# Residual added in PSUM by matmuls with the identity, output stored by half rows

## What is computed

```
h = h + peer_ffn(rmsnorm(h, norm_ffn_g), w_q, subkeys, u, v)
out = rmsnorm(h, norm_final_g)

peer_ffn(x): scores of x @ w_q against two sets of 128 subkeys; top 16 of each;
             top 16 of their 256 sums -> experts, g = softmax(top scores)
             act[t,h,k] = gelu(x[t] . u[expert]) * g[t,h,k]
             y[t]       = sum over h,k of act[t,h,k] * v[expert]
rmsnorm(x, g): x * rsqrt(mean(x*x) + 1e-6) * g
```

## Time and profile before

| | |
|---|---|
| median of 3 runs | 2017.38 us (2014.5 to 2019.98) |
| profiled execution | 2018.92 us |
| its span in the profile | 2017.1 us |
| mean granted clock of TensorE | 0.983 |
| PE busy | 1955.8 us, 97% |
| DVE, ACT, POOL busy | 1341.7 (67%), 1011.5 (50%), 320.5 us (16%) |
| loads | 311.4 MB read, 155 GB/s over the span |

### The profile page before, as it was taken

The page is one execution under the profiler, slowest core; times in us unless marked ns, Lnnn a source line. Parts: engine busy times, 40 slices in busy tenths (PEclk is TensorE's granted clock), DMA queues, the critical chain, the costliest instruction groups (busy, mean ns, idle before and its releaser), DMA issues.

```text
span 2017.1 us, 34435 instructions
## 1 busy us (share of the span) xinstructions
PE 1955.8 (97%) x12338; PEld 1730.1 (86%) x12338; DVE 1341.7 (67%) x2732; ACT 1011.5 (50%) x1641; POOL 320.5 (16%) x138
## 2 busy tenths in 40 slices
PE   7998999999999999999999999999999999999998
PEld 6776787778778888999899999999999998888886
DVE  6357556656655558889787689933666766666666
ACT  5436546555554446666434455665444443333333
POOL 0000000000000000000000057886666610000000
PEclk9898999999999999999999999999999999999999
DMA  5242454433345553433333534454343445555554
GB/s 229 73 157 74 149 211 172 174 117 128 115 145 189 186 184 130 147 136 136 106 126 126 178 126 168 179 180 151 138 146 136 143 162 188 197 190 195 191 194 156
DMA packets 85150, 313.99 MB, mean 156 GB/s; under 512 B 9456, under 2 KB 9456, under 8 KB 84592
## 3 DMA queue, kind: packets, MB, share of 16 engines
q1 hardware_dynamic: 85040, 312.49, 44.2%
HBM read 311.40 MB, written 1.05 MB: 155 GB/s over the span
## 4 chain that ended last, share of the span: by engine, by line
PE 92%; DVE 5%; ACT 2%; issue 1%; DMA 1%; SPq 0%; DVEq 0%; ACTq 0%
PE ps L282 29%; PE ps L414 22%; PE ps L401 15%; PE ps L1783 5%; PE ps L2635 3%; PE ps L2341 3%; PE ps L736 2%; PE ps L1852 2%; PE ps L430 1%; PE ps L799 1%; DVE wsplit L266 1%; PE ps L810 1%; PE ps L2172 1%; PE ps L2160 1%; PE ps L2155 1%
## 5 line engine op out<-in xcount | busy, mean ns | idle before, releaser
L260 ACT ACTIVATE wsplit<-ring 128x1024 fp32r<-128x1024 f32 x572 | 603.9, 1057 | 478.4 <-PE ps L414 268.9
L266 DVE TENSOR_TENSOR wsplit<-ring,wsplit 128x1024 fp32r<-128x1024 f32 x438 | 535.0, 1224 | 328.9 <-ACT wsplit L260 327.6
L282 PE MATMUL ps<-hsplit,wsplit 128*128 128x256 f32 x5064 | 648.2, 287 | 5.2 <-DVE hsplit L698 2.1
L282 PEld LDWEIGHTS ps<-hsplit,wsplit 128*128 128x128 f32 x5064 | 622.6, 193 | 12.9 <-issue 5.5
L266 POOL TENSOR_TENSOR wsplit<-ring,wsplit 128x1024 fp32r<-128x1024 f32 x134 | 320.3, 2397 | 1302.2 <-ACT wsplit L260 1302.2
L414 PE MATMUL ps<-wsplit,gsplit 128*128 128x512 f32 x1992 | 456.5, 390 | 0.0
L414 PEld LDWEIGHTS ps<-wsplit,gsplit 128*128 128x128 f32 x1992 | 373.3, 188 | 81.4 <-issue 4.2
L401 PE MATMUL ps<-wsplit,hsplit 128*128 128x512 f32 x1248 | 308.8, 405 | 17.6 <-DVE wsplit L266 10.5
L401 PEld LDWEIGHTS ps<-wsplit,hsplit 128*128 128x128 f32 x1248 | 241.3, 196 | 70.3 <-issue 18.9
L1783 PE MATMUL ps<-hsplit,wsplit 128*128 128x256 f32 x936 | 128.5, 288 | 0.0
L1783 PEld LDWEIGHTS ps<-hsplit,wsplit 128*128 128x128 f32 x936 | 116.3, 191 | 0.0
(11 more groups left out here) (319 smaller groups left out, 1706.5 us busy)
## 6 DMA issues: line engine op xcount, KB each, us to landing
ring<-in_weights SPq DMA_DIRECT2D x580, 512.0 KB, 3.3
work<-in_tables SPq DMA_DIRECT2D x1, 2123.0 KB, 12.4
xT<-in_x SPq DMA_DIRECT2D x1, 1024.0 KB, 4.9
work<-in_subkeys SPq DMA_DIRECT2D x1, 1024.0 KB, 15.0
work<-in_decay SPq DMA_DIRECT2D x2, 512.0 KB, 4.1
out_x<-work SPq DMA_DIRECT2D x2, 512.0 KB, 2.6
work<-in_w SPq DMA_DIRECT2D x1, 512.0 KB, 5.7
ring<-in_gain_row SPq DMA_DIRECT2D x1, 512.0 KB, 3.5
```

The costliest lines, as they stand in the source:

```text
L260: act.activation(wsplit[:, n % RING, 0, :], slab(s), ACT.Copy).then_inc(S("split", "lead"), 1)
L266: eng.tensor_tensor(wsplit[:, n % RING, 1, :], slab(s), wsplit[:, n % RING, 0, :], ALU.subtract).then_inc(S("split", RESTS[stream][0]), 1)
L282: mm = pe.matmul(dst, wsplit[:, n, a, c * P:(c + 1) * P], hsplit[:, b, c, :], start=(c == 0 and t == 0), stop=(c == KC - 1 and t == 2))
```

## The change

In words: the two functions that turn x in the query stage go, with the two waits on their result (of TensorE ahead of the early slabs, of VectorE ahead of its copies to PSUM) and the view `x_rows`. `residual_tensor` opens two banks with zeros, as before, and then adds x to them by 8 float32 matmuls of a chunk of `xT` (stationary) with the identity. For the second 128 tokens (banks 2 and 3) it waits only for the last GELU, for the first 128 (banks 0 and 1) for the last product of `late_vector`. The last norm reads PSUM in place of the sum in SBUF: ScalarE's Square waits for the matmuls directly, VectorE's scaled product reads `YR`. Each half row of 512 is stored by itself, as soon as its product is done.

```diff
--- before.py
+++ after.py
@@ -151,7 +151,6 @@
     picks = sb("picks", [P, 3, T])
     root, rinv = picks[:, 0, :], picks[:, 1, :]
     act_in, gated = sq[:, 0:3, :], sq[:, 3:6, :]
-    x_rows = xT[:, :, :].rearrange("p (t a) n -> p t (a n)", t=TT)
     row_stats = sb("row_stats", [P, 3, TT])
     bounds = sb("bounds", [P, 7, HH])
     lbd, lbe = bounds[:, 0:2, :], bounds[:, 2:4, :]
@@ -2457,8 +2456,6 @@
                 norm_tensor(pe, pre, 0)
             if u == 4:
                 column_tensor(pe, pre, 0)
-        pe.wait_ge(S("norm", "column"), rinv_steps(pre) + 3)
-        x_rows_tensor(pe, pre)
         score(0, 5)
         turn(1, 6, pre="m5")
         turn(2, 4)
@@ -2495,7 +2492,6 @@
             score(0, u - 1)
             if u == 1:
                 root_scalar(act, "n5", 0)
-        x_rows_scalar(act)
         score(0, 5)
         turn(1, 6)
         turn(2, 4)
@@ -2513,7 +2509,6 @@
         return 3 + c % 3
 
     def early_tensor(pe, st, stream):
-        pe.wait_ge(S("final", "x_rows"), 1)
         with pe.Fori(0, EARLY // 6) as i:
             for k in range(6):
                 split_project(pe, ps[:, hidden_bank(k), 0:T], stream, 16 + k, i).then_inc(S(st, "hidden"), 1)
@@ -2554,7 +2549,6 @@
         for tt in range(TT):
             own(v.tensor_scalar(best[:, tt, 0:6, :], best[:, tt, 0:6, :], row_stats[:, 2, tt:tt + 1], None, ALU.mult))
 
-        v.wait_ge(S("final", "x_rows"), 1)
         v.tensor_copy(ps_iota, iota)
         v.tensor_copy(ps_key, best_at[:, :, :, :].rearrange("p t h k -> p (t h k)"))
         own(v.tensor_copy(ps_best, best[:, :, :, :].rearrange("p t h k -> p (t h k)")))
@@ -2706,9 +2700,11 @@
             pe.wait_ge(S(st, "act"), i * 6 + (k + 1))
             split_rows_output(pe, st, VALUES + k, k % 3, i)
 
+
+        pe.wait_ge(S(st, "gelu"), NKEYS)
+        residual_tensor(pe, 1)
         pe.wait_ge(S(st, "late"), NKEYS - EARLY)
-        for y in range(4):
-            pe.matmul(ps[:, y, :], zeros[:, :], zero_rows(), start=True, stop=False, skip_group_check=True)
+        residual_tensor(pe, 0)
         with pe.Fori(0, TURNS) as i:
             for k in range(6):
                 output(k, i)
@@ -2734,42 +2730,32 @@
                 rest_of(v, st, VALUES + 2 + k, i)
         step(0, NKEYS - 1)
 
-
-
-    def x_rows_tensor(pe, pre):
-        wait_h(pe, pre)
-        for tt in range(TT):
-            for c in range(KC):
-                mm = pe.transpose(YR[:, tt, c * P:(c + 1) * P], xT[:, c, tt * P:(tt + 1) * P], eye)
-        mm.then_inc(S("final", "x_turned"), 1)
-
-    def x_rows_scalar(act):
-        act.wait_ge(S("final", "x_turned"), 1)
-        act.activation(x_rows[:, :, :], YR, ACT.Copy).then_inc(S("final", "x_rows"), 1)
-
+    def residual_tensor(pe, tt):
+        for half in range(2):
+            pe.matmul(ps[:, 2 * tt + half, :], zeros[:, :], zero_rows(), start=True, stop=False, skip_group_check=True)
+        for c in range(KC):
+            pe.matmul(YR[:, tt, c * P:(c + 1) * P], xT[:, c, tt * P:(tt + 1) * P], eye, start=False, stop=False,
+                      skip_group_check=True)
 
 
 
     def final_vector(v):
         steps = S("final", "vector")
-        for tt in range(TT):
-            v.wait_ge(S("rows", "tensor"), len(ROWS) * (TT + KC // 2) + tt + 1)
-            v.tensor_tensor(y_rows[:, tt, :], YR[:, tt, :], x_rows[:, tt, :], ALU.add).then_inc(steps, 1)
         slab_here(v, N_SLABS)
         for tt in range(TT):
             v.wait_ge(S("final", "scalar"), 2 * tt + 2)
             v.reciprocal(row_stats[:, 2, tt:tt + 1], row_stats[:, 1, tt:tt + 1]).then_inc(steps, 1)
-            v.wait_ge(steps, 3 + 3 * tt)
+            v.wait_ge(steps, 3 * tt + 1)
             for half in range(2):
                 c_ = slice(half * 512, (half + 1) * 512)
-                v.scalar_tensor_tensor(y_rows[:, tt, c_], y_rows[:, tt, c_], row_stats[:, 2, tt:tt + 1], slab(N_SLABS)[:, c_],
+                v.scalar_tensor_tensor(y_rows[:, tt, c_], YR[:, tt, c_], row_stats[:, 2, tt:tt + 1], slab(N_SLABS)[:, c_],
                                        ALU.mult, ALU.mult).then_inc(steps, 1)
 
     def final_scalar(act):
         act.preload_act_table(ACT.Sqrt)
         for tt in range(TT):
-            act.wait_ge(S("final", "vector"), tt + 1)
-            act.activation(sq[:, 4 * tt:4 * tt + 4, :].rearrange("p a n -> p (a n)"), y_rows[:, tt, :], ACT.Square,
+            act.wait_ge(S("rows", "tensor"), len(ROWS) * (TT + KC // 2) + tt + 1)
+            act.activation(sq[:, 4 * tt:4 * tt + 4, :].rearrange("p a n -> p (a n)"), YR[:, tt, :], ACT.Square,
                            accum_out=row_stats[:, 0, tt:tt + 1]).then_inc(S("final", "scalar"), 1)
             act.wait_ge(S("final", "scalar"), 2 * tt + 1)
             act.activation(row_stats[:, 1, tt:tt + 1], row_stats[:, 0, tt:tt + 1], ACT.Sqrt, scale=1.0 / D,
@@ -2842,9 +2828,11 @@
         sp.wait_ge(S("split", which), before + N_PEER - RING + 1)
         load_slab(N_SLABS, bass.AP(gain_row.tensor, gain_row.offset, [[0, P], [1, D]]))
         for tt in range(TT):
-            sp.wait_ge(S("final", "vector"), 3 + 3 * tt + 2)
-            sp.dma_start(out[:, tt, :], y_rows[:, tt, :]).then_inc(S("store", "out"), 16)
-        sp.wait_ge(S("store", "out"), 32)
+            for half in range(2):
+                c_ = slice(half * 512, (half + 1) * 512)
+                sp.wait_ge(S("final", "vector"), 3 * tt + 2 + half)
+                sp.dma_start(out[:, tt, c_], y_rows[:, tt, c_]).then_inc(S("store", "out"), 16)
+        sp.wait_ge(S("store", "out"), 64)
 
     @block.tensor
     def _(pe):
```

## The result

| | before | after |
|---|---|---|
| median, 20 runs each | 2021.36 us (2014.23 to 2025.12) | 2025.17 us (2018.56 to 2031.27) |
| ratio | | 1.0023, 95% interval 1.0013 to 1.0033 |
| profiled execution, its span | 2018.92, 2017.1 us | 2025.8, 2023.7 us |
| mean granted clock of TensorE | 0.983 | 0.982 |

By the ratio the changed kernel is slower by 0.23%, 4.6 us with an interval from 2.6 to 6.7; the two medians differ by 3.8. It is clear of noise and still under the 0.3% that the forecast took as its bound. The forecast for the difference was +3.25 us. The forecast time, 2020.6, was made from a median of three runs, 2017.38; with 20 runs the kernel before stands at 2021.36. So the measured 2025.17 lies outside the stated range of 2016.5 to 2024.5: of the 4.6 us between forecast time and measured time (the same figure as above by chance), 4.0 are the base and 0.6 is in the sum.

The account below looks back on a forecast made before the run. TensorE was taken as the bound, with 92% of the chain; +2.05 (middle), +3.1 (residual) and -1.9 (tail) gave +3.25 us on a median of 2017.38, so 2020.6 us, range 2016.5 to 2024.5.

Parts of the forecast that it names:

- the base: Whole run: time before the change, taken as 2017.38 us, to which the forecast difference was added.
- the sum: Whole change: middle +2.05, residual +3.1 and tail -1.9 us make +3.25 us, bounds -0.75 to +5.4; chance 0.42.
- the tail: After the last matmul: no add, Square from PSUM, half-size stores; -1.9 us, bounds -1.3 and -2.05.
- the residual: Behind the last GELU: 16 float32 matmuls cost 3.55, an earlier start credits 0.45; net +3.1 us.
- the collision: Query stage: POOL's earlier subtraction of slab 8 delays VectorE's piece 3, so TensorE waits; +2.05 us, bounds 0 and +2.4.
- The turn of x: Query stage: removing 16 transposes gains 0, as TensorE waits for piece 2 anyway; without that cover, 1.7 us.
- rival (a): Query stage: TensorE's clock falls while it does little, adding 1.85 us; together +5.1, 2022.5 us; chance 0.25.
- The store's -0.6: Within the tail: storing by halves leaves only 256 KB behind the last product; -0.6 us, bounds 0 and -0.75.

Follow-up runs that it names:

- e8: Changed kernel with the 16 transposes of x back, without ScalarE's copy: slab 5's query matmuls to the score behind slab 7 took 13.15 us (changed kernel 17.02).
- e2: Changed kernel with ScalarE's lead of slab 8 held until all four pieces are split: slab 5's query matmuls to the score behind slab 7, 14.63 us.
- e3: Changed kernel without the 16 residual matmuls: last GELU's start to first output matmul 1.82 us (changed kernel 5.27).
- e4: Changed kernel with one whole 512 KB store per 128 tokens: last two slabs' first matmul to end of span 11.76 us (changed kernel 11.71).
- e6: Changed kernel with 16 transposes of x replacing zero and residual matmuls (computed sum wrong): last GELU's start to first output matmul 2.14 us (changed kernel 5.27).
- e9: Changed kernel without the store of the third half row: last two slabs' first matmul to end of span 11.55 us (changed kernel 11.71).
- e10: Kernel before, with ScalarE's lead of slab 7 early and half of the turn of x ahead of its wait: ratio 0.9986 (0.9973 to 0.9998).
- e5: Changed kernel with ScalarE's lead of slab 7 before its copies of split h: slab 5's query matmuls to score behind slab 7, 11.16 us; timed ratio 1.0002.

## Why the prediction was right or wrong

Two steps failed. The base of the forecast time, a median of three runs, was 4.0 us too low, and that put the measured time outside the range. And in the sum of the change the clock stood at nothing, as a rival with a chance of 0.25, where the profile shows +1.83 us. The profiled pair differs by 3.86 + 3.42 - 1.31 = +5.97 us, against a sum of +3.25; the 2.72 us between them are the clock 1.83, the tail 0.59, the residual 0.32 and the collision -0.02.

- **The base.** Forecast as 2017.38 + 3.25. The median of three was 4.0 us below that of 20. The same code upstream of the query stage brings slab 5 between 1179.85 and 1187.86 us in the profiles here; that scatter belonged into the range of an absolute time, which I widened by 1 us only. Where the scatter comes from stays open.
- **The turn of x: credit 0.** Right. The second group of slab 6 starts when it did, to 0.01 us.
- **The collision: +2.05, measured +2.03.** The mechanism, the order at the port (piece 2, slab 8, piece 3) and the length of piece 3 (2.84 for "about 2.8") came out as worked out. The working said that ScalarE's copy was part of it; e8 shows that the transposes alone are enough.
- **The clock, rival (a).** This is the step of the mechanism that failed: left out of the sum, +1.83 in the profile. The clock fell in every profile without the transposes and without the early lead (after, e2, e3, e4, e6, e9) and in none with either. I weighed the waits for pieces 2 and 3 with one group of 6 matmuls between them. But the clock fell at 1194.5, before the wait for piece 3 began, and it fell in e2, which has no such wait. What came ahead of the fall was TensorE's wait of 1.49 us for score 5, which the 16 transposes I removed at no cost had filled in part, and then that of 1.52 us for piece 2; before, the two were 1.07 and 0.24 us. M rose by 3.86; (a) had given 2.05 + 1.85 = 3.90. That its 1.85 came out so near is partly luck, as the same code cost 1.29 to 1.96.
- **The residual: +3.1, measured +3.42.** The kind of row was right, its pace slightly off: the two groups of 8 take 1.99 and 1.80 us, together 3.79 for 3.55, and the four zero matmuls, now two and two, 1.06 instead of 0.97. The credit was 0.46 for 0.45.
- **The tail: -1.9, measured -1.31.** The add and its hand-over gave -1.30 as worked out. The store's -0.6 was 0, at its stated bound: I subtracted the time of the bytes from a landing time that hardly depends on them.
- **Sum.** +5.97 in the profiled pair, against +4.6 (2.6 to 6.7) by the ratio of the runs. That interval holds the forecast's +3.25 and rival (a)'s +5.1 alike: that (a) is what happened is told by the profiles, not by the times. Slower than before by less than 0.3%: as forecast.

## What to carry to other kernels

Before taking work off an engine at a point where it waits, ask what that work delays and what it keeps awake: here 16 transposes at no cost held back a lead by 1.3 us, so that POOL and VectorE did not meet, and kept TensorE's clock up. The exchange itself was poor: 3.4 us of matmuls on the engine that bounds the kernel for 1.3 us in the tail. The gain lay in lines that the change did not touch: one lead put into an idle microsecond of ScalarE, which frees VectorE from POOL (-2.0 us of M against the kernel before, in the changed kernel), and in e10 half of the turn moved ahead of the wait besides.

## What the runs showed of the hardware

VectorE and POOL took turns: the one that waits goes ahead of the next instruction of the other, in both directions: in the changed kernel VectorE's piece 2 came between POOL's slabs 7 and 8 (5.36 us for the two), and POOL's slab 8 between pieces 2 and 3. TensorE's clock went to half behind two idle stretches of 1.49 and 1.52 us with 1.4 us of work between them; in e4, with the same code, it went to half 0.4 us into the second stretch. It stayed at full with stretches of 1.07 and 0.24 us (before) and of 0.55 and 0.50 us (e5). In the changed kernel it came back at 1201.4, when TensorE had been busy without a gap since 1197.21. A store of 256 KB to the output landed 2.4 to 2.6 us after its issue, one of 512 KB 2.6 us.
